# Modulation chunks moved from the conditioning stage into the pooling stage, in column quarters

## What is computed

```python
def adaln(c, w, b):
    m = jnp.einsum('bd,de->be', jax.nn.silu(c), w) + b      # w: 1024 x 3072
    shift, scale, gate = jnp.split(m[:, None, :], 3, axis=-1)
    return shift, scale, gate

for l in range(DEPTH):
    shift, scale, gate = adaln(c, ada_w[l], ada_b[l])
    h = rmsnorm(x, pre_g[l]) * (1 + scale) + shift
    ...                     # layer 0: pooling mixer; layer 1: attention on shared K and V
    x = x + gate * rmsnorm(out, post_g[l])
```

## Time and profile before

| engine | busy us | share of the span |
|---|---|---|
| PE (matmul) | 2125.1 | 89% |
| PE weight load | 1865.5 | 78% |
| DVE | 906.3 | 38% |
| ACT | 763.2 | 32% |
| POOL | 693.5 | 29% |
| DMA | 312.8 MB, mean 132 GB/s | |

### The profile page before, as it was taken

The page is one execution under the profiler, slowest core; times in us unless marked ns, Lnnn a source line. Parts: engine busy times, 40 slices in busy tenths (PEclk is TensorE's granted clock), DMA queues, the critical chain, the costliest instruction groups (busy, mean ns, idle before and its releaser), DMA issues. The chain is left out here.

```text
span 2378.0 us, 33033 instructions
## 1 busy us (share of the span) xinstructions
PE 2125.1 (89%) x12939; PEld 1865.5 (78%) x12939; DVE 906.3 (38%) x1510; ACT 763.2 (32%) x1459; POOL 693.5 (29%) x512
## 2 busy tenths in 40 slices
PE   6969999999799924999999889999999999997692
PEld 1269999999799913999999867778788787876692
DVE  1332333344310066210000166555665655655305
ACT  2111111111212133100001135666666656655332
POOL 0123222333122214222233200444444444441122
PEclk9989999999899955999999889999999999999896
DMA  8621212121421041343333243665656656555404
GB/s 282 220 71 40 83 48 82 49 81 50 175 88 45 18 166 30 110 112 93 84 99 97 87 165 119 227 220 186 213 184 226 213 193 213 187 184 189 143 20 166
DMA packets 231052, 312.81 MB, mean 132 GB/s; under 512 B 39777, under 2 KB 165330, under 8 KB 230779
## 3 DMA queue, kind: packets, MB, share of 16 engines
q1 hardware_dynamic: 199251, 266.13, 34.9%
q10 hardware_dynamic: 31520, 44.50, 5.3%
q0 software_dynamic: 128, 0.07, 0.0%
HBM read 266.09 MB, written 44.57 MB: 131 GB/s over the span
## 5 line engine op out<-in xcount | busy, mean ns | idle before, releaser
L1276 POOL TENSOR_TENSOR Vl<-V,Vh 128x1024 fp32r<-128x1024 f32 x106 | 251.9, 2377 | 2.5 <-ACT Vh L1555 2.5
L121 PE MATMUL ps<-actH,w_hi_a 128*128 128x352 f32 x960 | 210.4, 327 | 3.4 <-DVE w_lo_a L92 3.4
L121 PE MATMUL ps<-actH,w_lo_a 128*128 128x352 f32 x960 | 207.8, 324 | 0.0
L121 PE MATMUL ps<-actL,w_hi_a 128*128 128x352 f32 x960 | 207.4, 324 | 0.0
L121 PE MATMUL ps<-actH,w_hi_c 128*128 128x352 f32 x792 | 173.3, 327 | 20.9 <-DVE w_lo_c L92 20.9
L1694 DVE TENSOR_TENSOR KTl<-ps,KTh 128x512 fp32r<-128x512 f32 x256 | 164.5, 685 | 54.3 <-ACT KTh L1561 52.7
L121 PE MATMUL ps<-actH,w_lo_c 128*128 128x352 f32 x792 | 171.5, 324 | 0.0
L121 PE MATMUL ps<-actL,w_hi_c 128*128 128x352 f32 x792 | 171.4, 325 | 0.0
L121 PEld LDWEIGHTS ps<-actH,w_hi_a 128*128 128x128 f32 x960 | 163.4, 190 | 3.8 <-DVE w_lo_a L92 3.7
L1561 ACT CAST KTh<-ps 128x512 fp32r<-128x512 f32 x256 | 137.4, 588 | 89.5 <-PE ps L1428 86.9
L121 PEld LDWEIGHTS ps<-actH,w_lo_a 128*128 128x128 f32 x960 | 165.5, 189 | 0.0
(11 more groups left out here) (267 smaller groups left out, 3833.8 us busy)
## 6 DMA issues: line engine op xcount, KB each, us to landing
K<-in_cache_k_dram SPq DMA_DIRECT2D x128, 512.0 KB, 3.3
V<-in_cache_v_dram SPq DMA_DIRECT2D x114, 512.0 KB, 3.4
adaw<-in_ada_w_dram SPq DMA_DIRECT2D x12, 2048.0 KB, 8.5
w_raw_a<-in_a_in_w_dram SPq DMA_DIRECT2D x32, 512.0 KB
g_d<-g ACTq DMA_DIRECT2D x16, 528.0 KB, 2.7
mov_b<-g_d SPq DMA_DIRECT2D x16, 528.0 KB, 5.8
w_raw_b<-in_a_out_w_dram SPq DMA_DIRECT2D x16, 512.0 KB
w_raw_c<-in_kv_w_dram SPq DMA_DIRECT2D x16, 512.0 KB
```

The source lines that it names most:

```text
L121: mm = pe.matmul(acc[:, c, 0:CH], wt[:, j % SPL, k, :], act[:, k0 + k, c * CH:(c + 1) * CH], start=first and k == 0 and s == 0, stop=last ...
L1276: eng.tensor_tensor(Vl[:, t % VR], places[t][0], Vh[:, t % VR].bitcast(F32), ALU.subtract).then_inc(s_Vl[t % VR], 1)
```

## The change

The conditioning stage keeps only the first four chunks (layer 0, shift and scale). The normed transpose follows behind all of them. The remaining 8 chunks (layer 0's gate, all of layer 1) become 16 of 256 columns (AW), 1 MB each, done in the pooling stage: four in each group, on PE behind the products of jobs 7 to 10 (m, z, z, m), and each is finished behind the product that follows.

In both stages the multiplication goes by column quarters: `scT` is widened to 32 columns (23 zero), and the k tiles are dealt out to four quarters of the array, quarter q writing PSUM partitions 32q to 32q + 31. The four partial sums are added by the multiplication that turns the result: instead of a transpose, `mrow` (now 128 partitions) is multiplied by `sel` (128 x 9, one where the partition is x modulo 32). `adab` is zero outside its nine rows. Gates are taken by `sel` as the stationary side and stored by SP.

In the conditioning stage SP issues x's first half, chunk 0, x's second half, the sample rows and chunk 1, and only then `preg`, `kvg`, `asc` and the biases. Some 40 lines of declarations and arena moves are left out.

```diff
+    def condition(pe, acc_bank, wide, chunk):
+        for k in range(KD // NQ):
+            for q in range(NQ):
+                mm = pe.matmul(ps[q * QD:(q + 1) * QD, acc_bank, 0:wide], scT[:, k * NQ + q, :],
+                               chunk[:, k * NQ + q, :], start=(k == 0), stop=(k == KD // NQ - 1))
+        return mm
...
     def stage_conditioning():
...
                 sp.dma_start(crow[1:NCOND, :], c_sample).then_inc(s_c, 16)
+                sp.dma_start(x_tok[:, 0:QB // 2, :], x_p[:, 0:QB // 2, :]).then_inc(s_x[0], 16)
+                sp.dma_start(adaw[:, 0], w_tiles(ada_w[0], 0, KD, 0, BANK)).then_inc(s_aw[0], 16)
+                sp.dma_start(x_tok[:, QB // 2:QB, :], x_p[:, QB // 2:QB, :]).then_inc(s_x[1], 16)
+                sp.dma_start(x_tok[0:NS, QB, :], x_s).then_inc(s_x[2], 16)
+                sp.dma_start(adaw[:, 1], w_tiles(ada_w[0], 0, KD, BANK, BANK)).then_inc(s_aw[1], 16)
...
-                for j, (l, n) in enumerate(chunks):
+                sp.wait_ge(s_abz, 1)
+                for j, c0 in enumerate(chunks):
                     if j >= 2:
                         sp.wait_ge(s_m, j - 1)
                         sp.wait_ge(s_mrow, j - 1)
...
-                    for k in range(KD):
-                        mm = pe.matmul(ps[0:NCOND, 6 + j % 2, :], scT[:, k, :], adaw[:, j % 2, k, :],
-                                       start=(k == 0), stop=(k == KD - 1))
-                    mm.then_inc(s_m, 1)
...
-                    if j >= FIRST:
-                        normed.pe(pe, x_tok, s_xn, lambda i: i + 1, *rounds_after(j))
+                    condition(pe, 6 + j % 2, BANK, adaw[:, j % 2]).then_inc(s_m, 1)
+                    pe.wait_ge(s_mrow, j + 1)
+                    if j:
+                        pe.wait_ge(s_mod, j)
+                    for i in range(BANK // P):
+                        mm = pe.matmul(ps[:, 5, i * NCOND:(i + 1) * NCOND], mrow[:, j % 2, i * P:(i + 1) * P],
+                                       sel[:, :], start=True, stop=True)
+                    mm.then_inc(s_mT, 1)
+                normed.pe(pe, x_tok, s_xn, lambda i: i + 1)
...
     def stage_pooling():
...
+        late = [(l, c) for l in range(2) for c in range(0, 3 * D, AW) if l or c >= GATE]
+        PER = len(kinds) // NG
+        at_job = {PER * gr + n: 4 * gr + n - 7 for gr in range(NG) for n in range(7, 11)}
...
+                def load_ada(c):
+                    l, c0 = late[c]
+                    if c >= 2:
+                        sp.wait_ge(s_m, c - 1)
+                    sp.dma_start(adaw[:, c % 2], w_tiles(ada_w[l], 0, KD, c0, AW)).then_inc(s_aw[c % 2], 16)
+                    if c:
+                        sp.wait_ge(s_mrow, c)
+                    sp.dma_start(adab[0:NCOND, :], ada_b[l:l + 1, c0:c0 + AW].broadcast_to(
+                        [NCOND, AW])).then_inc(s_ab, 16)
...
+                for j, src in enumerate(jobs):
+                    stream_weight(sp, w, j, src)
+                    if j - 1 in at_job:
+                        load_ada(at_job[j - 1])
+                    c = at_job.get(j - 3)
+                    if c in gates:
+                        store_gate(c)
...
+                def finish_ada(c):
+                    l, c0 = late[c]
+                    pe.wait_ge(s_mrow, c + 1)
+                    if c0 >= GATE:
+                        mm = pe.matmul(ps[0:NCOND, 7, 0:AW], sel[:, :], mrow[:, :], start=True, stop=True)
+                    else:
+                        for i in range(AW // P):
+                            mm = pe.matmul(ps[:, 7, i * NCOND:(i + 1) * NCOND], mrow[:, i * P:(i + 1) * P], sel[:, :],
+                                           start=True, stop=True)
+                    mm.then_inc(s_mT, 1)
...
+                def start_ada(c):
+                    pe.wait_ge(s_aw[c % 2], 16 * (c // 2 + 1))
+                    condition(pe, 6, AW, adaw[:, c % 2]).then_inc(s_m, 1)
...
+                    if n - 1 in at_job:
+                        if at_job[n - 1]:
+                            pe.wait_ge(s_mod, at_job[n - 1])
+                        finish_ada(at_job[n - 1])
+                    if n in at_job:
+                        if n % PER == 7:
+                            pe.wait_ge(s_pkfree, 2 * (gr + 1) * GT)
+                            pe.wait_ge(s_hU, (gr + 1) * GT)
+                        start_ada(at_job[n])
...
+                    if n in at_job:
+                        c = at_job[n]
+                        dve.wait_ge(s_m, c + 1)
+                        dve.wait_ge(s_ab, 16 * (c + 1))
+                        dve.tensor_tensor(mrow[:, :], ps[:, 6, 0:AW], adab[:, :], ALU.add).then_inc(s_mrow, 1)
```

More of the change, by code:

```diff
@@ L207, in build @@
     ident = keep.take("ident", [P, P])
+    sel = keep.take("sel", [P, NCOND])
+    scT = keep.take("scT", [P, KD, QD])
+    preg = keep.take("preg", [P, 2, KD])
     modA = keep.take("modA", [P, 2, KD, NCOND])
@@ L369, in stage_conditioning @@
         srow = a.take("srow", [NCOND, D])
[L370 to L373, removed]
+        adab = a.take("adab", [P, 2, BANK])
+        mrow = a.take("mrow", [P, 2, BANK])
         x_tok = a.take("x_tok1", [P, TT, D])
@@ L463, in _ @@
                 pe.wait_ge(s_scT, 1)
-                turned = 0
-                for j, (l, n) in enumerate(chunks):
+                pe.wait_ge(s_sel, 1)
+                for j in range(len(chunks)):
                     pe.wait_ge(s_aw[j % 2], 16 * (j // 2 + 1))
@@ L493, in _, with modulation @@
-                for j, (l, n) in enumerate(chunks):
+                dve.wait_ge(s_scz, 1)
+                dve.tensor_copy(scT[:, :, 0:NCOND],
+                                ps[:, 4, 0:KD * NCOND].rearrange("p (k c) -> p k c", k=KD)).then_inc(s_scT, 1)
+                def modulation(j):
+                    c0 = chunks[j]
                     dve.wait_ge(s_m, j + 1)
                     dve.wait_ge(s_ab[j % 2], 16 * (j // 2 + 1))
[L496 to L519, removed]
-                        link(dve, dve.reciprocal(rstd[:, :], rstd[:, :]))
-                        for i in range(TT):
-                            r = rows_of(i)
-                            dve.tensor_scalar(x_tok[0:r, i, :], x_tok[0:r, i, :], rstd[0:r, i:i + 1], None,
-                                              ALU.mult).then_inc(s_xn, 1)
-                        dve.wait_ge(s_mod, turned)
-                    if j >= FIRST:
-                        normed.dve(dve, link, *rounds_after(j))
@@ new lines, in modulation @@
+                    if j >= 2:
+                        dve.wait_ge(s_mT, j - 1)
+                    dve.tensor_tensor(mrow[:, j % 2], ps[:, 6 + j % 2, :], adab[:, j % 2], ALU.add).then_inc(s_mrow, 1)
+                    dve.wait_ge(s_mT, j + 1)
+                    if j == D // BANK:
+                        dve.wait_ge(s_small, 48)
+                    for i in range(BANK // P):
+                        ins = modulate(dve, ps[:, 5, i * NCOND:(i + 1) * NCOND], 0, c0, i)
+                    ins.then_inc(s_mod, 1)
@@ L532, in stage_pooling @@
+                modulation(3)
+                dve.wait_ge(s_mod, len(chunks))
+                normed.dve(dve, link)
     def stage_pooling():
```

118 lines of the change are left out of this document (74 added, 44 removed).

## The result

The kernel after takes 2356.95 us (2351.86 to 2357.04) against 2382.05 for the kernel before on the same chip: a ratio of 0.9887, interval 0.9871 to 0.9902. Run twice more beside other kernels it took 2350.1 (0.9861, 0.9844 to 0.9877) and 2352.7 (0.9878, 0.9862 to 0.9895). The change gains 25 to 33 us. The profiled execution of after has a span of 2354.4, 23.6 less than before.

A forecast was written before the change was run, and what follows sets the result against it. It took PE to bound pooling (busy 474.6 of 479.1 us). Terms -53 (first stage), +40 (pooling) and +1 (end) gave -12 us: span 2366 plus 3, so 2369 us, range 2343 to 2396.

The forecast's parts named there:

- What bounds the kernel: First-stage time removed is gained one for one; time put on PE between pooling products is lost one for one.
- First stage: Conditioning stage with four chunks: hands over at 77 us (9 slots) or 73 (4), against 130.1; saves 53 or 57.
- case (c): Chunk matmuls in pooling: neighbouring quarters overlap partly, 9 slots, 1.93 us a chunk; chance 0.47.
- case (b): Chunk matmuls in pooling: four quarters side by side without limit, 4 slots, 0.86 us a chunk; chance 0.26.
- The condition: A chunk's 8 matmuls on PE in pooling: records start in order, so 9 slots, 1.93 us, 16 times.
- The change of tiling: Turning the column tiling on and off in pooling: 0.1 us a chunk, bounds 0 and 0.33.
- The finish: Finishing a chunk on PE in pooling, by sel: 0.44 us a chunk.
- What else moves: DVE, PSUM, POOL and SP's queue in pooling: no cost, chunk transfers fit by a microsecond; end of pooling +1 us.
- The end of pooling: Last gate chunk's copy and store: the next stage's first issue may come 1 us later.
- all four side by side: Rival for the chunk matmuls: saved 57, added 24, so -33, 2348 us; chance 0.26.
- The serial rival: Quarters run one after the other in condition: +19, 2400 us, or 2404 with a 0.33 drain a chunk; chance 0.16.

The follow-up runs named there:

- The second kernel above: The changed kernel with the quarters in the outer loop of condition, so each quarter's matmuls stand in a row: 2351.17 us, ratio 0.9870.
- The first and third kernels: The changed kernel with all k tiles in one quarter: 2402.33 us; the changed kernel with each condition done twice in pooling: 2366.44 us.

## Why the prediction came out as it did

A change of -12 us was forecast and -25 was measured, -23.6 in the profiled spans. Of these 11.6 us of difference, the first stage brought some 0.6 more than forecast, pooling cost 25.2 in place of 41, and behind pooling 4.7 were lost that no term stood for.

**What bounds the kernel: right.** PE's idle time in pooling did not change, and each us put there was paid; each taken from the first stage was gained.

**First stage: right in the sum, not in its parts.** Forecast 77 with case (c), 73 with case (b); measured 76.41, and case (b) is what the chip does. mrow 0 waited for its bias until 30.27, as worked out (30.4). But the last modulation was written at 53.05, where 51 was worked out for four slots: the multiplication by `sel` took 1.88 us at the lower clock, where the four transposes of before had kept DVE for 0.50. Chunks 1, 2 and 3 all start right behind such a multiplication (32.83, 39.09 and 46.05), so chunk 3 waited for it and not for its transfer, as the chain had it. The rounds and tail then took 23.4 us for 22. These 3.4 us too few happened to stand against 4 too many for the slots.

**The condition: the step that failed.** "The second record of a quarter must wait for the first; only then can the next quarter's first one start beside it", and so nine slots, 1.93 us. I had taken the order in which the trace of before shows records, all of one and the same tile, for an order that the engine must keep between different tiles. It was no evidence for that: where every record uses the same tile, a free and a strict engine leave the same trace. The second kernel above shows that the order in the program doesn't matter, and 0.86 us that four slots are all. 16 x 1.07 = 17 us of the sum were mis-sized by this step. "For it: nothing in the trace" was true of case (b), and was as true of (c).

The Trainium skill, "TensorE: Matmul & The Clock Gate", Part 3, says that weight loads overlap with running matmuls only where the row group differs (its paragraph on the mechanism also lets a load into the background weight buffer be pulled ahead), and that matmuls start strictly in program order. The four quarters share their rows, and the loads at 15.93 and 16.78 start inside running matmuls: without that exception the first rule does not hold here. The second does not hold for the quarters, since with a quarter's records in a row in the program the period is the same to 0.02 us. The 2.38x of Part 3 was measured with three column tiles; four gave 3.44 / 0.87, some 4 times, here, the "Up to 4×" of the Trainium skill, "TensorEngine Tiling (Array Packing)", Overview.

**The change of tiling: mis-sized.** 0.1 us was taken, with bounds 0 and 0.33; it is 0.33, the upper one. 16 x 0.23 = 4 us. The first and third kernels show that it belongs to the edge between wide and narrow tiles, not to each matmul. The Trainium skill, "TensorEngine Tiling (Array Packing)", Key Properties, says that a change of tiling mode drains TensorE. The passage costs 0.33 us here; whether a drain is what takes it, no run shows.

**The finish: nearly right.** 0.44 was forecast; it is 0.40 for a gate chunk and 0.31 for the others. A gate's finish has `sel` with its 9 columns as the stationary side, so it is a narrow tile itself. Where a condition follows at once, the two share one passage. In the kernel that has layer 1's shift and scale back in the first stage, it stands alone before an m product, and that product's period is 6.54 (206.06 to 212.60) for 5.83: 0.71, its 0.43 and most of a passage.

**What else moves: right.** No transfer was late: the waits on `adaw` in after hold one entry, 9.9 us in the first stage, and the chunks of the pooling stage land in 6.5 us (median). The end of pooling came 0.6 us later behind its last g, for 1.

**Behind pooling** 28.3 us had been gained, and 23.6 arrived. 3.6 of the missing 4.7 lie at one place in attention's last loads: two issues of `K` and `V` 11.23 us apart in before (2173.46, 2184.69) are 14.84 apart in after (2145.97, 2160.81). The same gap is 11.2 in two of the experiments (quarters outer, quarters without the move) and 14.85 in all others, whichever way they were changed. What decides between the two was not tried. Nothing of the change is near, and I had no term for it.

The rival "all four side by side" at 2348 had the mechanism, and the time lies within the range because that reached to it. The three medians of after lie 2 to 9 us above it: 4 us are the change of tiling, and 4.7 were lost behind pooling, which brought the time nearer to the forecast by luck.

**The serial rival was the right one to fear.** With one quarter the kernel took 2402 us, close to the 2404 worked out with a drain of 0.33. That it decides from some 12 slots of 16 on was not tested: runs exist for 4 slots, where the move gains, and for 16, where it loses.

## What to carry to other kernels

A matmul with few stationary columns can be dealt out to the four column quarters, the partial sums added by the matmul that turns the result: a quarter of the time here, and some 0.33 us each time that the tiling changes, so chunks are better done in few large batches. An order that a trace shows among instructions that all compete for the same resource says nothing about instructions that don't; where two mechanisms leave the same rows, the chances between them should be nearly even. Before work is moved into a stage that is bound by the same engine, do it better where it stands and see what is left: the quarters in their old place brought 23 us, the quarters and the move 25 to 33.

## What the runs showed of the hardware that was not expected

- Fp32 matmuls of four column quarters run fully side by side: 16 records in four slots, 0.86 us for 8 matmuls of 256 columns and 3.64 us (with tail) for 8 of 512 at the lower clock, with 0.85 us from one slot to the next; at the higher one 1.95 in the kernel with the quarters outer. The order in the program changed the period by 0.02 us.
- 0.32 to 0.34 us for one passage from 128-column to 32-column stationary tiles and back, once per passage. Ahead of the second z product of a gate group, the finish (one quarter, 185.97) and the condition behind it (185.98) start within 0.01 us of each other.
- The column of the granted clock can read 1.00 where the records run at half pace: chunk 1 of after takes 3.64 us from 32.83 with 1.00 beside it, and chunk 3 of the kernel with the quarters outer 3.67 us from 45.06 with 0.50. The spacing of the records (0.85 or 0.43 us for 512 columns) tells the two levels apart.
- Three small vectors read element by element held SP's queue for 17.6 us (7.45, 9.60, 0.58) when they stood behind 8 MB of large transfers, where the first of them had been issued in 0.40 us at the head of the queue. Whatever stands behind such an issue waits for it; moving the biases ahead gave 3 us.
